# Scaling the eight input tiles of a state-space stage on VectorE alone, and on VectorE and GpSimd

## What is computed

```python
hp = _rmsnorm(xp, norm_mix[i])            # x * rsqrt(mean(x*x) + EPS) * g
op, re_p, im_p = _s5(hp, None, None, *w)

def _s5(h, h0_re, h0_im, a_re, a_im, log_dt, b_re, b_im, c_re, c_im, d, w_glu):
    ...
    bu = jnp.einsum('blgs,gps->blgp', u.astype(jnp.complex64), b_bar)
    _, states = lax.associative_scan(combine, (a_seq, bu), axis=1)
    ...
    y = jnp.real(jnp.einsum('gsp,blgp->blgs', c, states)).reshape(B, L, D)
    y = (y + d.astype(jnp.float32) * h.astype(jnp.float32)).astype(h.dtype)
    g = jax.nn.gelu(y)
    ab = g @ w_glu
    out = ab[..., :D] * jax.nn.sigmoid(ab[..., D:])
```

## Time and profile before

| | before |
|---|---|
| median of 3 runs | 1605.98 us (1603.01 to 1607.44) |
| the profiled execution | 1605.46 us |
| its span | 1603.6 us |
| its mean granted clock of TensorE | 0.965 |
| TensorE matmuls busy | 1515.2 us, 94% of the span |
| VectorE busy | 772.7 us, 48% |
| ScalarE busy | 602.1 us, 38% |
| GpSimd busy | 367.3 us, 23% |

### The profile page before, as it was taken

The page is one execution under the profiler, slowest core; times in us unless marked ns, Lnnn a source line. Parts: engine busy times, 40 slices in busy tenths (PEclk is TensorE's granted clock), DMA queues, the critical chain, the costliest instruction groups (busy, mean ns, idle before and its releaser), DMA issues.

```text
span 1603.6 us, 32114 instructions
## 1 busy us (share of the span) xinstructions
PE 1515.2 (94%) x11463; PEld 1426.4 (89%) x11463; DVE 772.7 (48%) x1226; ACT 602.1 (38%) x1085; POOL 367.3 (23%) x430
## 2 busy tenths in 40 slices
PE   5988999989999899999999999789999999999997
PEld 5957676678897899999999999679999999999997
DVE  3866556555554444442344454974444432344332
ACT  6344544475564333321133333342233311233223
POOL 0286675434321102200022133020012200022000
PEclk9979988899999999999999999889999999999998
DMA  7123223334334123222222466503323223222321
GB/s 176 24 57 96 87 81 91 97 91 117 105 88 130 40 80 91 79 82 89 78 79 78 147 181 161 201 13 88 90 69 90 80 80 90 76 83 78 92 67 59
DMA packets 245282, 147.62 MB, mean 92 GB/s; under 512 B 42071, under 2 KB 239614, under 8 KB 244190
## 3 DMA queue, kind: packets, MB, share of 16 engines
q1 hardware_dynamic: 237826, 138.35, 29.8%
q0 software_dynamic: 6704, 7.20, 1.9%
q10 hardware_dynamic: 684, 1.18, 0.2%
HBM read 128.42 MB, written 18.26 MB: 91 GB/s over the span
## 4 chain that ended last, share of the span: by engine, by line
PE 87%; DVE 7%; ACT 3%; issue 2%; DMA 1%; ACTq 0%; SPq 0%; DVEq 0%
PE bank L869 61%; PE bank L789 7%; PE bank L1127 3%; PE bank L932 3%; PE bank L1092 3%; PE bank L992 3%; PE bank L949 2%; PE bank L1004 1%; PE bank L980 1%; DVE arena_parts L1858 1%; DVE tmpa L2346 1%; DVE arena L2373 1%; DVE sq L2346 1%; ACT arena L1388 1%; PE bank L1095 0%
## 5 line engine op out<-in xcount | busy, mean ns | idle before, releaser
L869 PE MATMUL bank<-arena_parts,wR 128*128 128x288 f32 x4224 | 566.2, 295 | 6.7 <-ACT arena_parts L1465 3.7
L869 PEld LDWEIGHTS bank<-arena_parts,wR 128*128 128x128 f32 x4224 | 562.0, 188 | 8.9 <-issue 6.8
L869 PE MATMUL bank<-side_parts,wR 128*128 128x288 f32 x3360 | 447.4, 295 | 1.1 <-DVE tmpa L2418 1.1
L869 PEld LDWEIGHTS bank<-side_parts,wR 128*128 128x128 f32 x3360 | 445.5, 188 | 1.5 <-issue 1.3
L1872 DVE TENSOR_TENSOR wR<-wraw,wR 128x1024 fp32r<-128x1024 f32 x159 | 232.8, 1464 | 238.4 <-ACT wR L1451 237.0
L753 POOL TENSOR_TENSOR arena_parts<-sq,arena_parts 128x576 f32 x64 | 91.6, 1431 | 674.4 <-ACT arena_parts L1682 674.4
L1451 ACT ACTIVATE wR<-wraw 128x1024 fp32r<-128x1024 f32 x159 | 166.9, 1050 | 202.0 <-PE bank L869 187.6
L1388 ACT ACTIVATE arena<-bank 128x256 f32<-128x256 f32 (+9 forms) x223 | 95.5, 444 | 128.2 <-PE bank L789 74.4
L1679 ACT ACTIVATE tmpa<-bank 128x576 f32<-128x576 f32 x64 | 41.7, 651 | 195.5 <-PE bank L869 195.5
L2269 DVE TENSOR_TENSOR sq<-tmpa 128x576 f32<-128x576 f32 x64 | 48.6, 759 | 127.2 <-ACT tmpa L1679 127.2
L2197 DVE TENSOR_TENSOR kpR<-bank,rstd 128x576 f32<-128x576 f32 x32 | 24.2, 758 | 127.9 <-PE bank L869 127.9
(11 more groups left out here) (301 smaller groups left out, 1628.5 us busy)
## 6 DMA issues: line engine op xcount, KB each, us to landing
wraw<-in_mlp_w SPq DMA_DIRECT2D x128, 512.0 KB, 4.0
side<-in_cache_ckv SPq DMA_DIRECT2D x128, 128.0 KB, 2.1
wraw<-in_ssm_w_glu SPq DMA_DIRECT2D x16, 512.0 KB, 4.0
s_state_to_out<-side SPq DMA_DIRECT2D x16, 256.0 KB, 2.5
s_in_to_state<-yblk SPq DMA_DIRECT2D x8, 512.0 KB, 2.6
s_in_to_out<-side SPq DMA_DIRECT2D x64, 64.0 KB
wraw<-in_mla_w_o SPq DMA_DIRECT2D x8, 512.0 KB, 5.4
side<-s_in_to_state SPq DMA_DIRECT2D x2, 2048.0 KB, 12.9
```

What stands on the lines that cost most here:

```text
L869: return pe.matmul(bank[:, a, 0:HALF], wR[:, s, wp, k, :], tokens(k, xp)[:, a * HALF:(a + 1) * HALF], start=(first and j == 0), stop=(last ...
```

## The change

VectorE scales tiles 0 to 3. GpSimd scales tiles 4 to 7, after its store of tile 7 and before rest_of; it waits for the loads of tiles 0 to 5 and for the factors, and before tile 6 for the loads of tiles 6 and 7. The semaphore ones_set, which GpSimd had raised once for a tensor of ones, is now pool_made and counts on with each tile that GpSimd has scaled; TensorE waits for it at tiles 4 to 7.

```diff
-            pool.memset(ones[:, :], 1.0).then_inc(ones_set, 1)
+            pool.memset(ones[:, :], 1.0).then_inc(pool_made, 1)
...
+            pool.wait_ge(u_in[0], 16 * T * 6)
+            pool.wait_ge(rstd_ready, 3)
+            for k in range(KT // 2, KT):
+                if k == KT - 2:
+                    pool.wait_ge(u_in[1], 16 * T * 2)
+                u = U[:, 8 * k:8 * k + 8, :]
+                pool.tensor_tensor(u, u, rstd[:, 0:NC].unsqueeze(1).to_broadcast([P, 8, NC]), ALU.mult).then_inc(pool_made, 1)
+
             rest_of(R_GLU, zR[:, KT:, :, :])
...
-                    pe.wait_ge(ones_set, 1)
+                    pe.wait_ge(pool_made, 1)
...
             for k in range(KT):
-                pe.wait_ge(u_sb, k + 1)
+                pe.wait_ge(*((u_sb, k + 1) if k < KT // 2 else (pool_made, 1 + k - KT // 2 + 1)))
...
             def scale_input(k):
-                if k in (0, KT - 2):
-                    dve.wait_ge(u_in[k // 6], 16 * T * (6 if k == 0 else 2))
+                if k == 0:
+                    dve.wait_ge(u_in[0], 16 * T * 6)
...
-            for k in range(KT):
+            for k in range(KT // 2):
                 scale_input(k)
```

More of the change, by code:

```diff
@@ L257, in build @@
         HDR = nc.dram_tensor("s5_input", (D, T, NC), F32, kind="Internal").ap()
-        ones_set = sem("ones_set")
+        pool_made = sem("pool_made")
         waited = sem("waited")
```

## The result

With the change the median of 20 runs is 1608.76 us (1606.08 to 1610.55), before it is 1605.91 us over 20 runs (1599.16 to 1610.16). The ratio is 1.0018 with a 95% interval of 1.0010 to 1.0026: +2.85 us, between about 1.6 and 4.2. The prediction said 1607.8 us, +1.8, a small loss within 0.3% of no change, and that is where it lies. The profiled execution took 1608.27 us, its span 1606.1.

What follows compares the result with a forecast made beforehand. TensorE bounds the whole kernel (87% of the span), VectorE the stretch from scaling through the state groups. Four turns of 1.23 us against the shorter order net +1.82: 1605.98 + 1.82 = 1607.8 us, range 1603.0 to 1611.0.

Steps and rivals of the forecast that it cites:

- VectorE leads from the scaling to the end of group 3, and a shift of group 0 shifts all: State groups: nothing holds VectorE between scaling and groups' end; moving group 0's start moves 1051.09 and everything behind it equally.
- Four scalings less win 1.92 us, then ScalarE is late: Before group 0: four scalings end at 1007.35, ScalarE's copies of tile 0 at 1008.53, so group 0 starts 1.92 us earlier.
- Each product costs VectorE 1.23 us: Scalings and first products of group 0: each of four GpSimd products in between costs VectorE 1.91 - 0.68 = 1.23 us.
- two turns: VectorE and GpSimd alternate when both read SBUF; two were forecast among the scalings, two on the last scaling and group 0.
- The sum, +1.82: Group 0's start: effectively 1012.27 with four turns paid by VectorE, against 1010.45 before, a loss of 1.82 us.
- GpSimd's whole duration for each turn: SBUF reads, by the skill's harsher rule: each product blocks VectorE fully, four times 1.43 us, giving +2.6 us; not taken.
- the row: Profile stretch 1071 to 1079, both engines subtracting with two SBUF inputs, starts 1.91 us apart: the basis for 1.23 a turn.
- The sum counts from the first scaling: Scaling stage: the forecast counted group 0's start from 1004.62, where the profile before had VectorE's first scaling.
- The clock rivals: TensorE's chunk passes after group 3: a further slow pass, +4.90 us, chance 0.07; no clock fall, -1.26 us, chance 0.10.
- Nothing else costs: TensorE's wait for tiles 4 to 7 and the renamed semaphore cost nothing; the later matrix load has 9 us of cover.

Runs made afterwards that it cites:

- eight more: The changed kernel plus eight more GpSimd products on constant tensors, into tensors nobody reads: 1616.61 us against 1607.17 for the kernel before, ratio 1.0072.
- The kernel with the low parts on VectorE: Against the kernel before, VectorE makes all eight low-part subtractions ahead of output projection and gated unit, GpSimd none: 1600.22 against 1606.29 us, ratio 0.9955.

## Why the prediction was right, point by point

- *VectorE leads from the scaling to the end of group 3, and a shift of group 0 shifts all.* Right: the end of group 3 moved by 48.07 - 46.33 = 1.74 us, that of group 0 by 1.73, and each of the experiments that moved the one moved the other by the same to 0.1 us. That all behind group 3 moves by the same amount does not hold for single executions: the split came 71.70 us after the addition instead of 72.12, since the pair of passes was 1.3 us shorter.
- *Four scalings less win 1.92 us, then ScalarE is late.* Right: 1.90 with the products left out, with 1.17 us of idle time for ScalarE's copies.
- *Each product costs VectorE 1.23 us.* Right: the gaps between the starts of the scalings grew by 1.2 us twice (5.19 us for four instead of 2.77, two turns), and group 0's first four products took 1015.18 - 1011.26 = 3.9 us instead of 1.5, two turns. With eight more it was 1.13.
- *The sum, +1.82.* Against +1.74 in the stage. With GpSimd's whole duration for each turn the sum would have been +2.6; the trace is nearer to the row.
- *The sum counts from the first scaling, as it lay in one profile of before.* That this start can move, the prediction did not see. Before, group 0 hangs on the loads, which land 10.85 to 10.98 us after the addition to the residual; with the change it hangs on the factors. Where TensorE is quick at the sums of squares, the change gets the gain of that: its second profile ends group 0 at 20.89 us, its first at 19.97, and the difference is these rows of TensorE, first profile and second:

```profile
1002.13 2.78 PE L1280 MATMUL bank<-acc,side 128*128 128x72 f32 x16 [3.15 <-DVE acc L1852]
```

```profile
1002.45 3.69 PE L1280 MATMUL bank<-acc,side 128*128 128x72 f32 x16 [3.15 <-DVE acc L1852]
```

  The order of before does not get that gain. The kernel with the low parts on VectorE, which has this order, was as quick (first scaling 5.36 us after the addition), and VectorE only waited longer for the loads, so that group 0 ended at 19.49:

```profile
1006.81 1.43 DVE L2323 TENSOR_TENSOR hT<-hT,rstd 128x576 f32<-128x576 f32 x2 [1.87 <-DMA hT<-s_input]
```

  Measured from the addition the loss is thus 0.8 to 1.9 us.
- *The clock rivals.* The pair of passes was quicker with the change (5.53 us) than in the first profile of before (6.80), and before itself has 3.91 once. The change decides nothing there; as a spread of 3 us between executions it belongs in the range, not among the effects.
- *Nothing else costs.* Right as far as the runs show: TensorE never waited for GpSimd's tiles, and the second part of the matrices was not waited for. The median moved by 2.85 us, 1.1 more than the stage; its interval begins at 1.6, so this says nothing against 1.74, though it does not reach down to the 0.8 of the first profile. A further cause of about 1 us is neither shown nor excluded; the spread ahead of the output projection, 4 us in the profiles of before, could hide it.

## What to carry to other kernels

Work handed from VectorE to GpSimd is only cheap where the two do not read SBUF at the same time: here each product given away took 0.68 us of work from VectorE and cost it 1.2 us of waiting. Look for a stretch in which both already run, and compare their durations with those alone, before sharing; where sharing is wanted, give VectorE one operand in PSUM, or let GpSimd run while VectorE waits (the second was not tried by itself). And count from an event that the change cannot move: where a start hangs on a load in one version and on an engine in the other, one profile is too little.

## What was not expected of the hardware

A turn costs the instruction and not the elements: VectorE took 1.31 us for 128x4 beside GpSimd's products, 0.15 us without. GpSimd's product with a constant took 1.64 to 2.12 us beside VectorE, no less than that with two SBUF operands (1.41 to 1.94), yet stretched VectorE by 0.44 us each instead of 1.2; its fill (0.58 us) by nothing. And after the same 2.4 us of idle time TensorE was at the higher level in one execution of the kernel before (pair of passes 3.91 us, granted clock 1.00) and at the lower in another (first pass 3.66 us, granted clock 0.50):

```profile
1049.80:1053.70 3.90, 3.81 (x49) 3.51 (x49) 3.66 (x13) 0.00 (x0) 0.00 (x0) 1.00 0.02 4
```

```profile
1053.80:1057.40 3.60, 3.55 (x16) 3.30 (x16) 3.43 (x12) 0.00 (x0) 0.00 (x0) 0.50 0.00 0
```

These are the second and third profile's stretches over the pass (start and end, length, busy time of PE, PEld, DVE, ACT and POOL, granted clock, DMA share and GB/s); what decides between them was not tried.
